# Three re-orderings at stage borders of a two-block kernel: one transpose group, two gate tiles, the last sums and a store

## What is computed

```
h = modulate(rms_norm(x, norm_g[0]), ...)
x = x + 0.5 * gate * swiglu(h, ffn1_w_in, ffn1_w_out)

h = modulate(rms_norm(x, norm_g[1]), ...)
xp, q, k, v, z, b, a, g_pool, g_dn = split(h @ mix_w_in)
ya = pool_group_products(multiscale_pool(xp), pool_w) * pool_scale @ pool_proj
q, k, v = silu(causal_depthwise_conv(q, k, v))          # 8 heads of 128
o  = gated_delta_rule_chunked(l2norm(q), l2norm(k), v, ...)
yb = (rms_norm(o, dn_norm_g) * silu(z)) @ dn_proj
x  = x + gate * ((sigmoid(g_pool) * ya + sigmoid(g_dn) * yb) @ mix_w_out)

h = modulate(rms_norm(x, norm_g[2]), ...)
x = x + 0.5 * gate * swiglu(h, ffn2_w_in, ffn2_w_out)
return rms_norm(x, final_g)
```

## Time and profile before

| | us |
|---|---|
| three runs | 1977.80, 1982.19, 1983.47 |
| median | 1982.19 |
| the profiled execution | 1982.89 |
| its span in the trace | 1981.2 |
| PE busy in the span | 1936.3 (98%) |
| DVE, ACT, POOL busy | 1008.8, 738.2, 191.5 |

### The profile page before, as it was taken

The page is one execution under the profiler, slowest core; times in us unless marked ns, Lnnn a source line. Parts: engine busy times, 40 slices in busy tenths (PEclk is TensorE's granted clock), DMA queues, the critical chain, the costliest instruction groups (busy, mean ns, idle before and its releaser), DMA issues.

```text
span 1981.2 us, 25807 instructions
## 1 busy us (share of the span) xinstructions
PE 1936.3 (98%) x9544; PEld 1588.3 (80%) x9544; DVE 1008.8 (51%) x1409; ACT 738.2 (37%) x1291; POOL 191.5 (10%) x242
## 2 busy tenths in 40 slices
PE   6999999999999999999999999999999999999998
PEld 5888878766688888888887788898788888888887
DVE  6688866575454563333334666444543473333332
ACT  3345243465532342223222664343423342322332
POOL 1101110000000000000011235035000000000010
PEclk9999999999999999999999999999999999999999
DMA  8967922311043323333333232211334323333331
GB/s 301 310 176 222 316 64 88 85 33 44 23 116 113 100 86 99 92 104 90 98 88 108 75 96 80 67 46 31 87 95 126 112 81 112 95 96 93 95 97 56
DMA packets 330902, 212.87 MB, mean 107 GB/s; under 512 B 21374, under 2 KB 315451, under 8 KB 330303
## 3 DMA queue, kind: packets, MB, share of 16 engines
q1 hardware_dynamic: 319296, 170.58, 30.1%
q0 software_dynamic: 10368, 37.75, 5.4%
q10 hardware_dynamic: 1150, 3.35, 0.5%
HBM read 204.31 MB, written 7.35 MB: 107 GB/s over the span
## 4 chain that ended last, share of the span: by engine, by line
PE 91%; DVE 4%; DMA 2%; ACT 1%; issue 1%; ACTq 0%; POOL 0%; DVEq 0%; POOLq 0%
PE psum L434 26%; PE psum L436 25%; PE psum L435 25%; PE psum L1423 2%; DMA ada_w<-in_ada_w 1%; DVE ada_sum L2166 1%; PE psum L1207 1%; PE psum L1239 1%; PE psum L1220 1%; DVE delta_qkv_T L2166 1%; PE psum L1105 1%; PE psum L1121 1%; PE psum L1311 1%; PE psum L1369 1%; PE psum L957 1%
## 5 line engine op out<-in xcount | busy, mean ns | idle before, releaser
L434 PE MATMUL psum<-act_hi,w_hi 128*128 128x512 f32 x1616 | 648.9, 402 | 4.8 <-DVE act_lo L2166 2.5
L436 PE MATMUL psum<-act_hi,w_lo 128*128 128x512 f32 x1616 | 632.1, 391 | 0.0
L435 PE MATMUL psum<-act_lo,w_hi 128*128 128x512 f32 x1616 | 631.6, 391 | 0.0
L393 DVE TENSOR_TENSOR w_lo<-w_raw,w_hi 128x1024 fp32r<-128x1024 f32 x306 | 382.4, 1252 | 329.0 <-ACT w_hi L385 307.2
L385 ACT ACTIVATE w_hi<-w_raw 128x1024 fp32r<-128x1024 f32 x306 | 319.5, 1051 | 186.4 <-PE psum L436 179.0
L434 PEld LDWEIGHTS psum<-act_hi,w_hi 128*128 128x128 f32 x1616 | 304.7, 189 | 83.5 <-issue 19.6
L436 PEld LDWEIGHTS psum<-act_hi,w_lo 128*128 128x128 f32 x1616 | 304.5, 188 | 65.3
L435 PEld LDWEIGHTS psum<-act_lo,w_hi 128*128 128x128 f32 x1616 | 304.8, 189 | 61.3 <-issue 1.5
L731 POOL TENSOR_TENSOR squares<-squares 128x512 f32<-128x512 f32 x18 | 29.0, 1611 | 1254.1 <-ACT squares L1615 1254.1
L434 PE MATMUL psum<-ffn_hi,w_hi 128*128 128x512 f32 (+1 forms) x374 | 143.3, 383 | 0.0
L436 PE MATMUL psum<-ffn_hi,w_lo 128*128 128x512 f32 (+1 forms) x374 | 142.7, 382 | 0.0
(11 more groups left out here) (366 smaller groups left out, 2349.5 us busy)
## 6 DMA issues: line engine op xcount, KB each, us to landing
w_raw<-in_ffn_w_in SPq DMA_DIRECT2D x88, 512.0 KB, 3.8
ada_w<-in_ada_w POOLq DMA_DIRECT2D x72, 512.0 KB, 5.5
w_raw<-in_w_in SPq DMA_DIRECT2D x68, 512.0 KB, 4.0
w_raw<-in_mix_w_in SPq DMA_DIRECT2D x52, 512.0 KB, 3.8
w_raw<-in_ffn_w_out SPq DMA_DIRECT2D x32, 512.0 KB, 4.1
w_raw<-in_ffn_w_out SPq DMA_DIRECT2D x16, 384.0 KB, 3.4
w_raw<-in_w_branch_a SPq DMA_DIRECT2D x8, 512.0 KB, 4.0
w_raw<-in_w_out SPq DMA_DIRECT2D x8, 512.0 KB, 4.0
```

What stands on the lines that cost most here:

```text
L393: dve.tensor_tensor(WLO[:, n % 4, :], RAW[:, n % 4, :], WHI[:, n % 4, :].bitcast(F32), ALU.subtract).then_inc(w_lo, 1)
L434: pe.matmul(out, whi, hhi, start=start, stop=False)
L435: pe.matmul(out, whi, hlo, start=False, stop=False)
L436: return pe.matmul(out, wlo, hhi, start=False, stop=stop)
```

## The change

Four edits in three places.

1. `turn(23)` no longer stands ahead of the chunk loop. It is put between the second and the third quarter of the loop's first dense tile (`side_place(0)`), behind the key transposes.
2. The first two gate tiles of the merge (pass 0, f = 0, q = 0 and 1) are taken out of `merge_stage`: the first quarter of the first one stands ahead of `outputs_back(3)`, its other three quarters behind, then come the third and fourth pool products, then the second gate tile. `merge_stage` skips those two and makes its first pass outside the loop.
3. `last_sums` is cut in two parts. In the second half, part 0 (the sums of the older squares) stands between the second and the third chunk of the dense half, and only part 1 is left behind it.
4. The store of token group 3 is issued by ACT behind its own scaling, no longer by SP; SP's last store moves up one place.

```diff
@@ SP
-            for n in (2, 3):
-                sp.wait_ge(sem("out_T_taken" if n == 2 else "final_x"), KD + 2)
-                sp.dma_start(ov[:, n, 0:D - P], YTOK2[:, n, 0:D - P]).then_inc(stored, 16)
+            sp.wait_ge(sem("out_T_taken"), KD + 2)
+            sp.dma_start(ov[:, 2, 0:D - P], YTOK2[:, 2, 0:D - P]).then_inc(stored, 16)
@@ merge_stage
-                def body(pl):
+                def body(pl, first=False):
                     for f in range(2):
                         for q, (kts, rh, rl) in enumerate(((8, HHI, HLO), (8, HHI, HLO), (ka, ahi, alo), (kb, bhi, blo))):
-                            if q == 2 and f == 0:
+                            if first and f == 0 and q < 2:
+                                continue
+                            if first and f == 0 and q == 2:
                                 pe.wait_ge(u_lo, UNITS[name])
                             pe_tile(pe, pl, 4 * f + q, 4 * f + q, kts, rh, rl)
-                stage(name, body)
+                body(Place(name, 0), first=True)
+                with pe.Fori(1, INFO[name]["iters"]) as i:
+                    body(Place(name, i))
@@ last_sums, last_tile
+                if part == 0:
+                    pe.wait_ge(sem("squares_added"), 6 * 3)
+                    if half:
+                        pe.wait_ge(sem("mean_recip"), NT + 4)
+                else:
+                    pe.wait_ge(sem("squares_ready"), NT + 8 * 4 + half)
...
                         elif c == 0 and half:
-                            last_sums(0)
+                            last_sums(0, 0)
+                            last_sums(0, 1)
+                        elif c == 1:
+                            last_sums(1, 0)
                     mm.then_inc(chunk_done, 1)
-                last_sums(1)
+                last_sums(1, 1)
@@ between the convolution tiles and the chunk loop
-            turn(23)
...
-                beside(3 * c)
+                if c:
+                    beside(3 * c)
+                else:
+                    pl, k = side_place(0)
+                    quarter(pl, k, 0)
+                    quarter(pl, k, 1)
+                    turn(23)
+                    quarter(pl, k, 2)
+                    quarter(pl, k, 3)
@@ pool products
                 elif g == 2:
+                    quarter(Place("merge2", 0), 0, 0)
                     outputs_back(NT - 1)
+                    for q in range(1, 4):
+                        quarter(Place("merge2", 0), 0, q)
                     pe.wait_ge(sem("o_T_taken"), 8)
                 pe.matmul(PS[:, 4 + g, :], PLW[:, g, :], waiting(g), start=True, stop=True).then_inc(sem("pool_sum"), 1)
+            for q in range(4):
+                quarter(Place("merge2", 0), 1, q)
@@ ACT, last_taken
                 copy(YTOK2[:, 3, 0:D - P], YTOK2[:, 3, 0:D - P], scale=col(RCOL + 3)).then_inc(sem("final_x"), 1)
+                act.wait_ge(sem("final_x"), KD + 2)
+                act.dma_start(out[0, 3 * P:4 * P, 0:D - P], YTOK2[:, 3, 0:D - P]).then_inc(stored, 16)
```

More of the change, by code:

```diff
@@ L993, in out_back, with last_sums @@
                 mm.then_inc(sem("out_T"), 1)
[L995 to L1005, removed]
+            def last_sums(half, part):
+                if part == 0:
[4 more added lines that the diff above has]
+                    pe.wait_ge(sem("squares_ready"), NT + 8 * 4 + half)
+                slot = square_slot(4, KD - 1) if part else 0
+                for n in (0, 1):
+                    tok = slice((2 * half + n) * P, (2 * half + n) * P + P)
+                    mm = pe.matmul(PS[:, 4, 2 * half + n:2 * half + n + 1], SQ[:, slot, tok], ONES[:, 0:1],
+                                   start=(part == 0 and n == 0), stop=(part == 1 and n == 1))
+                if part == 0:
+                    return
                 mm.then_inc(sem("square_sum"), 1)
```

## The result

| | median us | lowest to highest us | executions |
|---|---|---|---|
| before | 1982.59 | 1977.80 to 1985.00 | 20 |
| changed kernel | 1984.32 | 1980.59 to 1987.32 | 20 |

The ratio of after to before is 1.0013, with a 95% interval of 1.0007 to 1.0019. In time that is +2.6 us (1.4 to 3.8), and by the medians alone +1.7 us. The change makes the kernel a little slower, by less than the 0.3% that the prediction called the limit of what a measurement can tell. With twenty executions of each kernel the interval leaves out 1, so that limit was set too wide. The forecast was 1984.1 us, from 1979.6 to 1987.4, with "within 0.3%" as the likeliest class. The profiled execution has a span of 1982.3 us, where the one before had 1981.2.

What follows compares the result with a forecast made beforehand. PE was taken to bound the kernel, busy 98% of the span. The terms +0.45 - 0.35 + 1.7 + 0.1 + 0 = +1.9 us on the median 1982.19 gave 1984.1 us, range 1979.6 to 1987.4.

Steps and rivals of the forecast that it cites:

- within 0.3%: Whole kernel: time differs from before by less than 5.9 us, the stated limit of measurement; chance 0.94.
- Part 1: Border to the chunk loop: keys still wait for inverse_less, turn(23)'s transposes cost +0.45 us in dense work (0 to 0.5).
- The rival by which the keys begin 0.8 us earlier: Border to the chunk loop: moving turn(23) frees the key transposes, sum +1.1, 1983.3 us; chance 0.07.
- Part 2: Ahead of the third merge tile: waits gather into one of 3.8 us set by DVE's chain; gain -0.35 us.
- the gap is really filled: Third merge tile: PE not held by DVE, gains the whole 4.1 us, sum -3.6, 1978.6 us; chance 0.04.
- The clock: Uncovered dense work behind the long wait at the third merge tile: lowered clock costs +1.7 us (0 to 3.4).
- rival without a lowered clock: Behind the wait at the third merge tile: clock stays at 1.00, sum +0.2, 1982.4 us; chance 0.15.
- Parts 3 and 4: Kernel's end: splitting the last sums costs +0.1 us (-0.4 to +0.2); ACT's store gives 0, at best -0.2.
- The part that it leaves open: Last stores: if the sequencer's issue time ends last, the store edit is worth 0.4 us, the whole 1983.7.
- The rival on the slower side: Behind both waits: clock lowered longer, 3.4 us lost in place of 1.7; +5.7 us, 1987.9 us; chance 0.06.

Runs made afterwards that it cites:

- early split: Changed kernel with ACT's and DVE's split of the merge's chunk 2 moved ahead of the pool stage's work; 1983.07 us, ratio 1.0011 to the kernel before.
- swapped tiles: Kernel before plus the gate-tile move and chunk 2 split early, with the yb_hi and pool_hi tiles swapped in each merge pass; 1977.83 us, ratio 0.9980.
- filler matmuls: Changed kernel plus twelve unread 128x512 matmuls in the wait ahead of the first tile that reads pool_hi; 1982.04 us, ratio 1.0003 to the kernel before.
- part 2 alone: Kernel before with only the merge's first two gate tiles moved around the output transposes and pool products; 1983.14 us, ratio 1.0000.
- third execution: Changed kernel run once more, nothing altered, beside the kernel before on the same chip; 1984.36 us, ratio 1.0014.
- parts alone: Kernel before with only the turn(23) move, only the gate tiles, or only the sums and store edits; 1982.07, 1983.14 and 1982.72 us.

## Why the prediction was right

The stated range also holds the time of the kernel before (1982.59), so the measured time alone would have told little. What supports the prediction is that each term of its sum and each of its signs was found in the traces.

**Part 1, +0.45 forecast, +0.49 and +0.48 measured.** The step held as it was written: the keys wait for `inverse_less`, and taking `turn(23)` out from ahead of them gave nothing, 4.30 us from the last inverse step to the keys in both kernels. The price of four transposes in dense work was read from another place of the kernel and fits to 0.04 us. The rival by which the keys begin 0.8 us earlier is out. `value_rows(7)`, which came later, held up nobody.

**Part 2, -0.35 forecast, -0.30 measured.** The wait changed its place: forecast 3.8 us in one piece ahead of the third merge tile, measured 3.60 and ended by `w_lo`, as forecast. Reading the ends of two engines against each other, instead of PE's waits alone, made this visible ahead of time: PE's two pauses of 2.0 us were real, but DVE's chain of 14 us was only half a microsecond shorter than all that PE did beside it. The early split shows that `w_lo` was the last link (1.25 us) and `pool_lo` the one before it, and the swapped tiles show that PE's own work would have allowed 4.07 us. The rival "the gap is really filled" had the right size; its condition is not met by the change, and is by that other order.

**The clock, +1.7 forecast (0 to 3.4), +1.5 to +2.8 measured.** This was the largest term and carried the sign. Its mechanism is shown by the filler matmuls: same start of the tile, clock at 1.00, and 1.38 us back by the `yb` tile. The traces of this case give 1.47, 1.63 (23.49 less 19.07, less the 2.79 of before) for part 2 alone, and 2.46 at the `yb` tile or 2.8 at the tile behind it for the third execution with the same wait. All are within the bounds, and none is near the 0 of the rival without a lowered clock. The value I took was the row of this very place in the kernel before, which is one draw from that spread, so its closeness to the first trace (1.7 to 1.47) is in part luck. The timed ratio, +2.6 us for the whole change, lies inside what the traces give: +0.49, -0.30 and 1.5 to 2.8 are +1.7 to +3.0.

**Parts 3 and 4, +0.1 and 0 forecast, 0.0 and 0.0 measured.** The four sums put into the dense half cost 0.46 us (the lag behind the old kernel grows from +1.04 to +1.50), and having only four left behind it saves 0.46 (it falls back to +1.04 at DVE's take-up). What the prediction passed over is PE's wait just behind the dense half: 1.13 us ahead of the last sums before and 1.08 after, until ACT has made the last square. The four older sums don't need that square. By my estimate, from these rows alone, they would fit into that wait, and the 0.4 us saved behind it (1.06 less 0.64) would be kept. No run here tried it. The last store was issued 0.48 us nearer to the scaling (1977.08 to 1978.17, where it was 1976.03 to 1977.60), and the span's end didn't move: from DVE's take-up to the end are 5.8 us in both kernels (1976.45 to 1982.3, and 1975.41 to 1981.2), with the DMA engines 0.94 busy at 350 GB/s, as before. The rule of the Trainium skill that the prediction weighed (DMA: Bandwidth & Descriptors, section Rules for kernel authors), that more issuing engines bring no bandwidth, agrees with this row. The part that it leaves open, 0.4 us of issue time, did not appear.

**What was not right.** The rival on the slower side, a long lowered stretch behind both waits, was given 0.06. Something near one half of it did occur in one of three executions, behind the second wait: 2.8 us lost, where the rival had 3.4. Behind the first one the granted clock over the five microseconds from the key transposes is 0.66 or 0.67 in all nine traces, whether the pause ahead was 1.44 and 0.16 us or 2.25 in one piece, and the distance from the keys to the first pool product gives no more than part 1's transposes. That the ratio gives +2.6 us and the first trace +1.7 would fit a share of executions with the long stretch, but the interval (1.4 to 3.8) holds both. How often it comes stays open: three traces of the 3.6 us wait, two with the short stretch and one with the long, don't give a frequency. The forecast in time was also near by some luck: it was built on a median of three executions (1982.19), and the twenty give 1982.59, while the shift itself was forecast at +1.9 and measured at +2.6. Nor do the timed ratios of the parts alone (0.9999, 1.0000 and 0.9999) add up to 1.0013; their intervals of about 0.001 each are wide enough for both.

## What to carry to other kernels

Where another engine's chain ends last, moving work into PE's waits can simply gather them in one place further on, as it did here. Ask first which engine's chain ends last there, and give PE something long that doesn't need the end of that chain. Here an order in which PE takes the operand that is ready first, together with the early split, was worth 4 us, and filling the pauses alone cost 1.1 to 2.5 (28.90 and 30.25 less 27.76). And the lowered clock behind the old waits ran under cover of DVE's chain and set nothing; once the wait stood at the head of uncovered dense work, the clock behind it had to be paid. Look also for the wait right beside the place to which work is moved: the last sums went into full dense work, with 1.1 us of waiting just behind it.

## What the runs showed of the hardware that I had not expected

The loss of clock behind one and the same wait isn't one number. Behind 3.60, 3.61 and 3.62 us of waiting, twelve dense steps took 4.26, 4.42 and 5.25 us, where 2.79 were due; behind 2.35 us they took 4.46. So in its one trace the shorter wait bought no clock. With twelve matmuls of no use in the wait, and 0.90 us of it left, the clock stayed at 1.00, and the median on the same chip was 2.3 us lower (1984.36 to 1982.04), though the intervals of the two ratios overlap.
